# Two mixer layers: decay rows as one product of two parts, half a weight piece between small products, earlier small weights, another order at layer 1's start, another bank

## The reference

```python
z = rms_norm(h, norm1_g[l]) @ w_in[l]
y = concatenate([mlstm_mixer(...), mla_mixer(...), gla_mixer(...), conformer_conv(...)], axis=-1)
h = h + group_rms_norm(y, fuse_g[l], N_GROUPS) @ w_out[l]
u = rms_norm(h, norm2_g[l])
f = swiglu(u, ...) if l % 2 == 0 else moe_ffn(u, ...)
h = h + f
```

```python
log_d = where(causal, b[..., :, None] - b[..., None, :] + ic[..., None, :], -inf)
m_t = maximum(b + m[..., None], max(log_d, axis=-1))
s = einsum('bhtd,bhjd->bhtj', qc, kc) * exp(log_d - m_t[..., None])
```

## Time and profile before

| | us |
|---|---|
| median of 3 runs | 1236.68 (1235.75 to 1237.65) |
| the profiled execution | 1236.0 |
| its span | 1234.2 |
| PE busy | 1214.1 (98%) |
| DVE, ACT, POOL busy | 945.3, 837.9, 192.0 |
| mean granted clock of TensorE | 0.995 |

### The profile page before, as it was taken

The page is one execution under the profiler, slowest core; times in us unless marked ns, Lnnn a source line. Parts: engine busy times, 40 slices in busy tenths (PEclk is TensorE's granted clock), DMA queues, the critical chain, the costliest instruction groups (busy, mean ns, idle before and its releaser), DMA issues.

```text
span 1234.2 us, 17123 instructions
## 1 busy us (share of the span) xinstructions
PE 1214.1 (98%) x5976; PEld 1012.1 (82%) x5976; DVE 945.3 (77%) x901; ACT 837.9 (68%) x889; POOL 192.0 (16%) x229
## 2 busy tenths in 40 slices
PE   7999999999999999999999999999999999999997
PEld 7888888888888878888888888888888888888885
DVE  5765554455485569998888989889889988888987
ACT  7667644344766757777677777777767768777776
POOL 9864200000486430000000000000000000000000
PEclk9999999999999999999999999999999999999998
DMA  9522976525253299999999999999999999999971
GB/s 307 184 104 73 398 280 204 176 79 171 72 161 120 85 347 365 359 336 384 363 353 376 366 354 367 375 344 369 376 350 365 375 352 360 382 348 360 396 266 53
DMA packets 171221, 353.48 MB, mean 286 GB/s; under 512 B 13875, under 2 KB 44741, under 8 KB 171168
## 3 DMA queue, kind: packets, MB, share of 16 engines
q1 hardware_dynamic: 167600, 344.17, 78.0%
q0 software_dynamic: 3392, 8.34, 2.0%
q10 hardware_dynamic: 176, 0.27, 0.1%
HBM read 347.78 MB, written 6.82 MB: 287 GB/s over the span
## 4 chain that ended last, share of the span: by engine, by line
PE 95%; DVE 2%; ACT 1%; DMA 1%; issue 0%; SPq 0%; DVEq 0%; ACTq 0%
PE bank L1830 16%; PE bank L1832 16%; PE bank L1831 16%; PE bank L1850 7%; PE bank L1848 7%; PE bank L1849 7%; PE bank L1874 2%; PE bank L1794 2%; PE bank L1795 2%; PE bank L1796 2%; PE bank L1975 2%; PE bank L1976 2%; PE bank L1977 2%; DVE low L1233 1%; PE bank L2316 1%; PE bank L2040 1%
## 5 line engine op out<-in xcount | busy, mean ns | idle before, releaser
L1233 DVE TENSOR_TENSOR low<-ring,high 128x2048 fp32r<-128x2048 f32 (+1 forms) x302 | 686.6, 2287 | 126.1 <-ACT high L774 122.6
L774 ACT ACTIVATE high<-ring 128x2048 fp32r<-128x2048 f32 (+1 forms) x327 | 624.4, 1913 | 174.2 <-PE bank L1832 116.5
L1830 PE MATMUL bank<-high,uTh 128*128 128x512 f32 x880 | 349.0, 397 | 1.2 <-DVE low L1233 1.0
L1832 PE MATMUL bank<-high,uTl 128*128 128x512 f32 x880 | 343.1, 390 | 0.0
L1831 PE MATMUL bank<-low,uTh 128*128 128x512 f32 x880 | 342.9, 390 | 0.0
L1830 PEld LDWEIGHTS bank<-high,uTh 128*128 128x128 f32 x880 | 165.2, 188 | 40.3 <-DVE low L1233 5.6
L1832 PEld LDWEIGHTS bank<-high,uTl 128*128 128x128 f32 x880 | 165.2, 188 | 35.4
L1831 PEld LDWEIGHTS bank<-low,uTh 128*128 128x128 f32 x880 | 165.4, 188 | 32.4
L1848 PE MATMUL bank<-high,moe_hTh 128*128 128x512 f32 x320 | 125.3, 392 | 0.0
L1850 PE MATMUL bank<-high,moe_hTl 128*128 128x512 f32 x320 | 124.6, 390 | 0.0
L1849 PE MATMUL bank<-low,moe_hTh 128*128 128x512 f32 x320 | 124.5, 389 | 0.0
(11 more groups left out here) (412 smaller groups left out, 1433.9 us busy)
## 6 DMA issues: line engine op xcount, KB each, us to landing
ring<-in_moe_w_up_dram SPq DMA_DIRECT2D x176, 512.0 KB, 6.1
ring<-in_moe_w_gate_dram SPq DMA_DIRECT2D x176, 512.0 KB, 5.8
ring<-in_moe_w_down_dram SPq DMA_DIRECT2D x176, 512.0 KB, 6.2
ring<-in_w_in_dram SPq DMA_DIRECT2D x36, 512.0 KB, 6.2
ring<-in_ffn_w_up_dram SPq DMA_DIRECT2D x22, 512.0 KB, 5.0
ring<-in_ffn_w_gate_dram SPq DMA_DIRECT2D x22, 512.0 KB, 5.3
ring<-in_ffn_w_down_dram SPq DMA_DIRECT2D x22, 512.0 KB, 4.2
ring<-in_w_out_dram SPq DMA_DIRECT2D x16, 512.0 KB, 3.7
```

The lines of the kernel that those rows point to most:

```text
L774: act.activation(high[:, n % SPLIT, 0:width], slot(n)[:, 0:width], ACT.Copy).then_inc(s["high_ready"], 1)
L1233: dve.tensor_tensor(low[:, n % SPLIT, 0:width], slot(n)[:, 0:width], high[:, n % SPLIT, 0:width].bitcast(F32), ALU.subtract).then_inc(s["l ...
L1830: pe.matmul(o, ah, bh, start=(kd == 0), stop=False)
L1832: last = pe.matmul(o, al, bh, start=False, stop=(kd == KD - 1))
```

## The change

It does seven things, in both layers where nothing else is said:
- `decay`: `negm` has 64 partitions in fp32r, with minus `mrun` rounded in rows 0 to 3 and the rest of it in rows 32 to 35 (DVE), zeros elsewhere (ACT). `head_rows` picks both rows of a head, so that one fp32r product of 256 columns and one of 128 replace three float32 ones of 128. The mask comes last.
- DVE adds `mrun` to `cumf`, and two transposes replace four float32 products for bank 4.
- The first half of gqk stands ahead of `decay(0)`, the second behind `decay(1)`; ACT takes the exponentials of the first scores ahead of the two decays.
- The second fuse transposes use bank 4 in place of bank 0.
- Layer 0: POOL issues the small weights' DMAs ahead of the angles.
- Layer 1, piece b: ACT writes `high` in two halves, the first one ahead of the second tile's gains; POOL writes the first half of `low`, DVE the second.
- Layer 1, DVE: the second tile's sum stands between the halves of the first tile's gains.

```diff
@@ -180,7 +180,8 @@
-            negm = sb("negm", [4, S], F32, part)
...
+            negm = sb("negm", [64, S], F32R, part)
@@ -222,6 +223,7 @@
+        head_rows = sb("head_rows", [64, 4], F32R)
...
@@ -344,7 +345,7 @@
-        FUSE_BANKS = (5, 0, 0, 0)
+        FUSE_BANKS = (5, 4, 0, 0)
...
@@ -629,7 +630,6 @@
-            angles()
@@ -657,11 +657,20 @@
+                    n = n0 + IN_AT["b"]
+                    pool.wait_ge(s["b_half"], 1)
+                    for c in range(0, PIECE // 2, 512):
+                        last = pool.tensor_tensor(low[:, n % SPLIT, c:c + 512], slot(n)[:, c:c + 512],
+                                                  high[:, n % SPLIT, c:c + 512].bitcast(F32), ALU.subtract)
+                    last.then_inc(s["b_half"], 1)
...
                 pool.dma_start(ukv[:, :], mla_w_ukv[l]).then_inc(s["ukv_in"], 16)
+                if l == 0:
+                    angles()
@@ -674,8 +683,7 @@
-                if l == 0:
-                    pool.wait_ge(s["sin_ready"], 1)
@@ -889,7 +897,12 @@
+                    n = n0 + IN_AT["b"]
+                    act.wait_ge(loaded[SLOT_OF[n]], 32 * FILL_OF[n])
+                    act.wait_ge(s["piece_used"], n - SPLIT + 1)
+                    act.activation(high[:, n % SPLIT, 0:PIECE // 2], slot(n)[:, 0:PIECE // 2], ACT.Copy).then_inc(s["b_half"], 1)
...
+                    act.activation(high[:, n % SPLIT, PIECE // 2:], slot(n)[:, PIECE // 2:], ACT.Copy).then_inc(s["high_ready"], 1)
@@ -901,10 +914,10 @@
                     split_in("l1")
-                split_in("b")
                 if l:
...
                 else:
+                    split_in("b")
                     act.wait_ge(s["consts"], 1)
@@ -947,7 +960,7 @@
                     act.wait_ge(s["ang_ready"], 1)
-                    act.activation(cossin[:, :, :, :], ang[:, :, :, :], ACT.Sin).then_inc(s["sin_ready"], 1)
+                    act.activation(cossin[:, :, :, :], ang[:, :, :, :], ACT.Sin)
                 act.preload_act_table_set(LN_EXP)
@@ -995,8 +1008,15 @@
+                if l == 0:
+                    chain.done(act.activation(head_rows[:, :], ones[0:64, 0:4], ACT.Copy, scale=0.0))
                 act.wait_ge(s["mcum_ready"], l + 1)
-                act.activation(negm[:, :], mrun[:, :], ACT.Copy, scale=-1.0).then_inc(s["negm_ready"], 1)
+                chain.done(act.activation(negm[:, :], ones[0:64, :], ACT.Copy, scale=0.0))
+                chain.wait()
+                if l == 0:
+                    for r in (0, 32):
+                        act.activation(head_rows[r:r + 4, :], ident[r:r + 4, r:r + 4], ACT.Copy)
+                act.activation(negm[0:4, :], mrun[:, :], ACT.Copy, scale=-1.0).then_inc(s["negm_ready"], 1)
                 act.wait_ge(s["mcol_tr"], l + 1)
@@ -1009,10 +1029,6 @@
-                act.wait_ge(s["mcol_ready"], l + 1)
-                decay(0)
-                decay(1)
@@ -1020,6 +1036,9 @@
                                               bias=smax[:, 0, hd:hd + 1], scale=scale, accum_out=psums[:, 0, hd:hd + 1]))
+                act.wait_ge(s["mcol_ready"], l + 1)
+                decay(0)
+                decay(1)
                 split_in("vo0")
@@ -1318,10 +1337,13 @@
                     split_in("l0")
-                    for t, sem, value in ((0, "dense_half", 1), (1, "piece_used", DENSE0 + N_FFN)):
-                        add_tile(t, DENSE_ACC[t], sem, value)
-                        normalize(l, t)
-                        tile_gains(3 * l, NORM1 + KD * l, t, START_BANKS[l])
+                    add_tile(0, DENSE_ACC[0], "dense_half", 1)
+                    normalize(l, 0)
+                    tile_gains(3 * l, NORM1 + KD * l, 0, START_BANKS[l], (0, 1))
+                    add_tile(1, DENSE_ACC[1], "piece_used", DENSE0 + N_FFN)
+                    tile_gains(3 * l, NORM1 + KD * l, 0, START_BANKS[l], (2, 3))
+                    normalize(l, 1)
+                    tile_gains(3 * l, NORM1 + KD * l, 1, START_BANKS[l])
                 else:
@@ -1340,9 +1362,16 @@
-                dve.wait_ge(s["low_ready"], n0 + IN_AT["b"])
-                split_in("b")
+                if l:
+                    n = n0 + IN_AT["b"]
+                    dve.wait_ge(s["low_ready"], n)
+                    dve.wait_ge(s["b_half"], 2)
+                    dve.wait_ge(s["high_ready"], n + 1)
+                    dve.tensor_tensor(low[:, n % SPLIT, PIECE // 2:], slot(n)[:, PIECE // 2:],
+                                      high[:, n % SPLIT, PIECE // 2:].bitcast(F32), ALU.subtract).then_inc(s["low_ready"], 1)
+                else:
+                    split_in("b")
                 if l == 0:
@@ -1404,7 +1433,9 @@
                 chain.wait()
-                dve.tensor_tensor_scan(mrun[:, :], aj[:, :], aj[:, :], 0.0, ALU.max, ALU.max).then_inc(s["mcum_ready"], 1)
+                chain.done(dve.tensor_tensor_scan(mrun[:, :], aj[:, :], aj[:, :], 0.0, ALU.max, ALU.max))
+                chain.wait()
+                dve.tensor_tensor(cumf[:, :], mrun[:, :], cumf[:, :], ALU.add).then_inc(s["mcum_ready"], 1)
@@ -1426,6 +1457,9 @@
                 conv_steps(8, 12)
+                dve.wait_ge(s["negm_ready"], 2 * l + 1)
+                dve.scalar_tensor_tensor(out=negm[32:36, :], in0=mrun[:, :], scalar=-1.0, in1=negm[0:4, :].bitcast(F32),
+                                         op0=ALU.mult, op1=ALU.subtract).then_inc(s["negm_ready"], 1)
@@ -1987,12 +2021,11 @@
                     claim(b, "dt_ready", HEADS * l + hd + 1)
-                    row = bc(ident[0:4, hd:hd + 1], [4, P])
+                    row = bc(head_rows[:, hd:hd + 1], [64, P])
+                    pe.matmul(bank[b][:, 0:S], row, negm[:, :], start=True, stop=False)
+                    pe.matmul(bank[b][:, S:S + P], row, negm[:, P:S], start=False, stop=False)
                     pe.matmul(bank[b][:, :].rearrange("p (a n) -> p a n", a=2)[:, :, 0:P], ident_r[:, :],
-                              bc(mask_kr[:, :].unsqueeze(1), [P, 2, P]), start=True, stop=False)
-                    pe.matmul(bank[b][:, 0:P], row, negm[:, 0:P], start=False, stop=False)
-                    pe.matmul(bank[b][:, P:S], row, negm[:, P:S], start=False, stop=False)
-                    pe.matmul(bank[b][:, S:S + P], row, negm[:, P:S], start=False, stop=True).then_inc(s["x_ready"], 1)
+                              bc(mask_kr[:, :].unsqueeze(1), [P, 2, P]), start=False, stop=True).then_inc(s["x_ready"], 1)
@@ -2116,8 +2149,7 @@
                 for t in range(TT):
-                    pe.matmul(bank[4][:, 8 + 4 * t:12 + 4 * t], mrun[:, t * P:(t + 1) * P], ident[0:4, 0:4], start=True, stop=False)
-                    last = pe.matmul(bank[4][:, 8 + 4 * t:12 + 4 * t], cumf[:, t * P:(t + 1) * P], ident[0:4, 0:4], start=False, stop=True)
+                    last = pe.transpose(bank[4][:, 8 + 4 * t:12 + 4 * t], cumf[:, t * P:(t + 1) * P], ident[0:4, 0:4])
                 last.then_inc(s["mcol_tr"], 1)
@@ -2138,10 +2170,11 @@
-                pe.wait_ge(s["negm_ready"], l + 1)
+                half("gqk", 0, "gqk_ready")
+                pe.wait_ge(s["negm_ready"], 2 * l + 2)
                 decay(0)
                 decay(1)
-                piece("gqk", "gqk_ready")
+                half("gqk", 1)
                 piece("rg0", ("grs_ready", l + 1))
```

More of the change, by code:

```diff
@@ L256, in build @@
         wslot = sb("wslot", [P, 1])
-        sb("pad_un", [P, 8])
         with ExitStack() as part:
@@ L375, in build @@
                 "x0_in", "x1_in", "ident_ready", "dense_half", "pos_in", "stage_zero", "norm1_in", "rows_in", "gateb_in", "ln_in", "router_in", "moe_g_in", "ukv_in", "final_in",
-                "consts", "cols_tr", "cols_ready", "ang_ready", "sin_ready",
+                "consts", "cols_tr", "cols_ready", "ang_ready", "b_half",
                 "high_ready", "low_ready", "piece_used",
```

## The result

The changed kernel took 1228.85 us in the median of nine runs (1227.08 to 1232.45), the kernel before 1236.14 (1235.72 to 1237.8): a ratio of 0.9945, with a 95% interval of 0.993 to 0.996. It is faster, by 7.3 us. The forecast was 1223.7, reaching from 1222.3 to 1225.2, and to 1227.8 with rivals 1 to 3: the median lies outside of both. The nine runs fall into three groups: three from 1227.1 to 1227.3 at a granted clock of 0.998, two at 1228.7 and 1228.9 (0.996 to 0.997), and four from 1232.0 to 1232.5 (0.993 to 0.994). The profiled execution, of 1227.17 us, is of the first.

The account below looks back on a forecast made before the run. PE was taken to bound the kernel (95% of the chain of waits), the experts passing shifts on unchanged. Gains of 13.0 us from 1236.0 gave 1223.0, plus 0.7 for the median: 1223.7 us, range 1222.3 to 1225.2.

Parts of the forecast that it names:

- rivals 1 to 3: Clock still falls (chance 0.15), a cover is too short (0.10), or new decays are not cheaper (0.06): 1221.8 to 1227.8 us.
- The cover of the addition: DVE's addition between the scan of mrun and mcum_ready, taken at nothing: PE wants bank 3 only after piece a.
- Rival 2: A cover is too short: layer 0's scan of gx meets POOL, or bank 6's margin fails; 1225.0 to 1226.5, chance 0.10.
- The decays: Eight decays, each 1.165 us before, 0.40 with three fp32r products: gain 6.1 us, bounds 2.4 to 6.4.
- The clock: Falls to 1.2 GHz in gqk behind the decays, 1.5 us in each layer, both go: gain 3.0 (0 to 3.1).
- rival 1: Clock still falls, behind the decays or at other small products; one costs 1.5, two 3.0: 1225.2 to 1226.7, chance 0.15.
- Columns for bank 4: Transposes replace float32 products that feed bank 4: gain 0.7 us in each layer, 1.4 in all (1.2 to 1.6).
- Small weights: Layer 0: DMAs issued earlier end L2074's idle 1.47 us, gates just in time: gain 1.4 us (0.8 to 1.5).
- Layer 1's start: PE's 0.66 us wait for low of b goes, the 0.80 for gains mostly stays: together 0.7 (0.4 to 1.0).
- The bank: Second fuse transposes no longer wait 0.27 us for DVE, bank 0's last reader: 0.5 us in both layers.
- ACT's margin: ACT takes two decays last; 0.9 us of margin left before rg0's first half would wait for bank 6.
- The sum: Decays 6.1, small weights 1.4, clock 3.0, columns 1.4, layer 1's start 0.7, bank 0.5, less 0.1: 13.0 us.

Follow-up runs that it names:

- The two ways of taking the wait away: Changed kernel with bank 3 released by the scan of mrun: 1224.7 us; or with POOL's layer 1 low of mk behind the scan of gx: 1224.17 us.
- two variants: Changed kernel with the old decays' products: 1232.52 us; changed kernel with gqk whole behind the two decays: 1230.07 us.

## Why the prediction was wrong, point by point

- **The cover of the addition, the step that failed.** I wrote that PE first wants `mcum_ready` at L2095 "with the piece a in between", and took the addition at nothing. In layer 0 that held (1.33 us, no wait). In layer 1 it cost 2.77 of waiting, 3.03 with what followed, and behind it the clock: 4.7 more in four of nine runs. The two at 1228.8 went with the wait too, but none of them was traced. Rival 2 named the collision with POOL and that two new operations could take part in it, but put it at the scan of `gx` and mq. I gave the operation no length and the piece a no rows as its cover, although rows 14 and 15 showed what POOL does to the one that stands there; and the operation that was added came ahead of that one, so it met POOL first. The two ways of taking the wait away gave back 2.5 and 3.0 us. With the first the kernel takes 1224.7, which lies in the range of the forecast, but in part by luck: the decays gave 2.3 less than forecast and other terms 1.6 more.
- **The decays.** 0.40 each was forecast, 0.69 measured, so 8 x 0.475 = 3.8 us in place of 6.1; with the old products put back it is 3.8 too. The fp32r pace of 0.12 that I used stands in rows of products of one height. The term that was too small is the change of height: 0.03 to 0.04 were allowed for it in a decay, and its two changes cost 0.34 (0.69 less the 0.35 with 128 rows).
- **The clock.** Behind the decays no fall came in the changed kernel's four traces, as forecast. One of my two reasons, the new decays, is borne out (with the old ones put back falls return in half of the runs), though not which of their properties it is; the other, gqk's half, is worth nothing. But the term of 3.0 took the kernel before at two falls and the changed one at none, and its wait brought a new one. This is rival 1's outcome, by idle time rather than by small products, and dearer than its 1.5: 4.7. What I held against the Trainium skill's rule ("TensorE: Matmul & The Clock Gate", section "What's actually happening"), that PE was busy ahead of the fall, is true of the decays' place (the old decays' trace too); at the kv products idle time came before the fall, as the rule has it. Neither accounts for both places.
- **Columns for bank 4.** 1.11 to 0.34 (54.10 to 54.44): 0.77 a layer, 1.5 in all; forecast 1.4.
- **Small weights.** The walpha product follows without idle time at 28.44, the gates at 29.07, and kv is 1.64 sooner, of which 0.13 were there at l0 (13.72 and 13.59), so 1.5; forecast 1.4.
- **Layer 1's start.** b has no wait, the 0.80 stays; 7.57 - 6.63 = 0.9 gained from l0 to kv; forecast 0.7.
- **The bank, and ACT's margin.** No wait at the second fuse transposes, and none at rg0; as forecast.
- **The sum.** By the experts' start it is 9.3 of the forecast 13.0: 3.0 lost at kv and 2.3 in the decays, while the other terms gave 1.6 more. Of these 0.6 are in the points above, with the 0.13 of l0. The starts in both traces tell where the remaining 1.0 is: 0.16 and 0.15 at the second fuse transposes, where PE comes 0.43 and 0.42 sooner and only waits of 0.27 were counted; 0.25 between there and the first transposes of layer 1, most of it in these, which now start when PE is free (0.17 behind the product ahead of them, 0.38 before); some 0.2 round the third and fourth decays of both layers; the rest in steps under 0.1. The runs with falls make the median 1.7 worse than the profiled execution. That the experts pass a shift on one to one was right: PE came 9.32 us sooner, and the span is 8.9 shorter.

## What to carry to other kernels

These are lessons of this one kernel. Price an operation that you add on DVE with the length that its neighbour has at that very place, POOL's work beside it included, and ask which release stands behind it: a count for a later reader should not hold a bank that the earlier step set free. Between small products try one height of rows, even if it takes zeros: here it halved a decay. A wait of some 3 us on TensorE is to be priced at up to 8 (3.03 and 4.7 here), since the clock may fall behind it, in some executions and not in others; so compare runs at like clocks, and look at all of them.

## What was not expected of the hardware

- A product whose stationary operand has another height than the one before (64 and 128 rows) gets its weights only at its own start; a decay of 64, 64, 128 rows took 0.69 us, one of 128, 128, 128 rows 0.35. The Trainium skill ("TensorE: Matmul & The Clock Gate", section "LDWEIGHTS (loading the stationary operand)") gives the load a time that does not hang on the rows. The loads' own lengths agree (0.18 and 0.19), but their place does not follow from it.
- A 4x256 addition on DVE took 0.41, 1.33 or 5.72 us, by what POOL did beside it.
- After 2.75 us of idle time the granted clock was 0.50 for 10.2 us, in three executions, at the same place; in a fourth it stayed at 1.00 after 2.77 us. After 3.31 us, ahead of all four kv products, the runs were some 1.5 us longer or not at all. In the traces of two variants it stayed at 1.00 as well (2.8 and 2.7 us). What decides between these is open. Also open is what made the kernel before spread by 5.5 us; its falls were traced in one execution only.
